# End of the first FFN: GpSimd's modulation-row additions and edge masks behind a new wait, the last rows scaled later

## The reference

```python
for i in range(DEPTH):
    mod_l = jnp.split((sc @ ada_w[i] + ada_b[i])[:, None, :], N_MOD, axis=-1)
    ...
    x = x + g_m * _rms_norm(y_lat, norm_post_mix[i])
    f_lat = _conv_ffn(_modulate(_rms_norm(x, norm_pre_ffn[i]), sh_f, sc_f),
                      ffn_w_up[i], ffn_conv_w[i], ffn_conv_b[i], ffn_w_down[i])
    x = x + g_f * _rms_norm(f_lat, norm_post_ffn[i])

def _conv_ffn(h, w_up, conv_w, conv_b, w_down):
    z = h @ w_up
    u, v = z[..., :D_FF], z[..., D_FF:]
    u = _dwconv(u, conv_w, conv_b, (1, 1))
    return (jax.nn.gelu(u) * v) @ w_down
```

## Time and profile before

| | |
|---|---|
| median of 3 runs | 1964.74 us (1964.59 to 1966.92) |
| profiled execution | 1965.58 us |
| its span | 1963.7 us |
| TensorE busy | 1923.5 us, 98% of the span |
| VectorE, GpSimd, ACT busy | 85%, 65%, 50% |

### The profile page before, as it was taken

The page is one execution under the profiler, slowest core; times in us unless marked ns, Lnnn a source line. Parts: engine busy times, 40 slices in busy tenths (PEclk is TensorE's granted clock), DMA queues, the critical chain, the costliest instruction groups (busy, mean ns, idle before and its releaser), DMA issues. The chain is left out here.

```text
span 1963.7 us, 28044 instructions
## 1 busy us (share of the span) xinstructions
PE 1923.5 (98%) x8838; PEld 1569.5 (80%) x8838; DVE 1661.0 (85%) x1752; ACT 991.1 (50%) x1417; POOL 1276.4 (65%) x858
## 2 busy tenths in 40 slices
PE   5999999999999999999999999999999999999999
PEld 3777776888888888888888789878888888888886
DVE  5688888879789889999989886897888888888887
ACT  5867678457444444445444456663434334333334
POOL 4534343665877788887778975475567655556765
PEclk9999999999999999999999999999999999999999
DMA  9322322541222232222332241111111111111114
GB/s 348 108 81 91 107 85 88 212 162 42 99 76 96 85 97 95 86 85 85 94 98 85 91 156 44 65 65 54 54 54 53 59 47 64 53 53 60 49 54 180
DMA packets 78017, 179.76 MB, mean 92 GB/s; under 512 B 5104, under 2 KB 28944, under 8 KB 77328
## 3 DMA queue, kind: packets, MB, share of 16 engines
q1 hardware_dynamic: 77968, 179.13, 26.9%
HBM read 166.52 MB, written 12.58 MB: 91 GB/s over the span
## 5 line engine op out<-in xcount | busy, mean ns | idle before, releaser
L2319 POOL TENSOR_TENSOR So_lo<-So_raw,So_hi 128x512 fp32r<-128x512 f32 x120 | 199.1, 1666 | 198.8 <-DVE So_raw L2962 167.7
L3026 DVE TENSOR_TENSOR Y<-Y,ps 128x1024 f32<-128x1024 f32 x280 | 324.2, 1208 | 3.3
L1836 ACT ACTIVATE So_hi<-So_raw 128x512 fp32r<-128x512 f32 x180 | 112.4, 624 | 148.2 <-POOL So_raw L2311 75.4
L2088 POOL TENSOR_TENSOR red<-red,E_quad 128x512 f32<-128x512 f32 x77 | 123.9, 1610 | 60.4 <-ACT E_quad L1890 57.5
L1836 ACT ACTIVATE WB_hi<-rawB 128x512 fp32r<-128x512 f32 x120 | 74.6, 629 | 166.0 <-PE ps L1258 111.8
L2041 POOL TENSOR_TENSOR WA_lo<-rawA,WA_hi 128x1024 fp32r<-128x1024 f32 x20 | 59.3, 2967 | 127.7 <-DVE u L2655 102.7
L1836 ACT ACTIVATE WA_hi<-rawA 128x512 fp32r<-128x512 f32 x120 | 73.1, 625 | 121.0 <-PE ps L1278 83.3
L1258 PE MATMUL ps<-T_hi,So_hi 128*128 128x512 f32 x336 | 131.3, 391 | 0.0
L1258 PE MATMUL ps<-T_hi,So_lo 128*128 128x512 f32 x336 | 130.8, 389 | 0.0
L1258 PE MATMUL ps<-H_hi,WA_hi 128*128 128x512 f32 x336 | 130.7, 389 | 0.0
L1258 PE MATMUL ps<-H_lo,WA_hi 128*128 128x512 f32 x336 | 130.7, 389 | 0.0
(11 more groups left out here) (445 smaller groups left out, 6270.6 us busy)
## 6 DMA issues: line engine op xcount, KB each, us to landing
rawA<-wA SPq DMA_DIRECT2D x62, 512.0 KB, 3.3
rawB<-wB SPq DMA_DIRECT2D x62, 512.0 KB, 3.4
E_quad<-ada SPq DMA_DIRECT2D x44, 512.0 KB, 3.5
quad<-ada SPq DMA_DIRECT2D x8, 2048.0 KB, 9.2
rawB<-wC SPq DMA_DIRECT2D x22, 512.0 KB, 3.7
rawA<-wC SPq DMA_DIRECT2D x20, 512.0 KB, 3.7
ada_first<-ada SPq DMA_DIRECT2D x8, 1024.0 KB, 14.9
outT<-X SPq DMA_DIRECT2D x16, 512.0 KB, 2.7
```

The costliest lines, as they stand in the source:

```text
L1836: A(dst[:, at:at + HF], op_source(name), ACT.Copy).then_inc(op_hi, 1)
L2088: TT(red[:], red[:], E_quad[:, :, k % 2 * P:k % 2 * P + P], ALU.add).then_inc(red_made, 1)
L2319: TT(lo[:, at:at + HF], op_source(name), hi[:, at:at + HF].bitcast(F32), ALU.subtract)\
L3026: TT(at, at, ps[:, bank:bank + 2, :], ALU.add).then_inc(d_added, 1)
```

## The change

On GpSimd (`last_step`), the first two additions of the last group (c = 2) wait for `last_ready` of the first half; the edge masks stay behind them. The other two (c = 3) are no longer in one piece behind the masks, but one each behind the two odd sums. On ACT, `scale_rows(PAIRS + 1, 3)` moves from behind the table load to behind the fourth square. On TensorE, `quad_columns` moves from behind n = 8 to behind n = 10.

```diff
@@ down_last (TensorE)
-                    if n == 8 and L == 0:
+                    if n == 10 and L == 0:
                         quad_columns(PAIRS + 1, ps[:, 3, 0:4])
                     if n == 10:
                         square_sums(q, 0)
@@ last_up (ACT)
                 act.preload_act_table(ACT.Sqrt)
-                if L == 0:
-                    scale_rows(PAIRS + 1, 3)
@@ ffn (ACT)
                 for n in range(2 * KT):
                     act.wait_ge(d_added, added + n + 1)
                     square(q, n // KT, n % KT, Y[:, n % KT, hs(n // KT)])
+                    if L == 0 and n == 3:
+                        scale_rows(PAIRS + 1, 3)
@@ add_rows (GpSimd)
-            def add_rows(q, c):
+            def add_rows(q, c, part=(0, 1)):
-                for k in (2 * c, 2 * c + 1):
+                for k in (2 * c + n for n in part):
@@ last_step (GpSimd)
                 if L == 0:
+                    pool.wait_ge(last_ready, 1)
                     add_rows(PAIRS + 1, 2)
                     window_edges()
-                    add_rows(PAIRS + 1, 3)
@@ ffn (GpSimd)
                 last_step(L)
                 q, i = 3 + 4 * L, 1 + 2 * L
-                odd_sums(q, 0)
+                for n, p in enumerate((3, 5)):
+                    odd_sum(q, 0, p)
+                    if L == 0:
+                        add_rows(PAIRS + 1, 3, (n,))
                 line_sums(q, 1, (1, 2, 3))
```

## The result

The changed kernel takes 1968.72 us (median of 20 runs, 1966.96 to 1971.47). The kernel before takes 1965.92 us in 20 runs beside it (1964.26 to 1967.71); the first three of them, shown ahead of the prediction, had a median 1.2 us lower, 1964.74. The ratio is 1.0013, 95% interval 1.0007 to 1.0019. The forecast was 1965.9, within 1963.6 to 1968.0. The sign was right, and the time lies 0.7 us outside the range.

What follows compares the result with a forecast made beforehand. TensorE, busy 1923.5 of 1963.7 us, was taken as the bound, so its idle or low-clock time decides. −1.2 (wait A) − 0.9 (quad_columns moved) + 3.3 (waiting before the sums) = +1.2 on 1964.74, giving 1965.9; range 1963.6 to 1968.0.

Steps and rivals of the forecast that it cites:

- Part 1: VectorE's gated product and second convolution, freed of GpSimd's additions, let TensorE start sooner: wait A falls by about 1.2 us.
- wait A: TensorE's 1.71 us idle before the first product with WB_hi, behind VectorE's convolution, gated product and remainder; to fall about 1.2.
- Part 2: TensorE finishes tiles 0 to 10 at 1134.9 instead of 1137.0, then waits for red's last addition (quad_columns) and last_sum.
- Part 3: GpSimd's queue starts 3.5 us later, its last addition directly ahead of VectorE's merge; last_sum at 1139.6, 1.2 us later.
- port shared by halves: Alternative to taking turns at SBUF: addition and merge would overlap, and merge would lose about 0.6 us instead of 1.2.
- Part 4: Behind last_sum: column sums at 1139.6 instead of 1138.4, then the same 1.6 us low-clock loss as before.
- Costs at nothing: Later pool_w load (ScalarE losing up to 2 us), X reload 3.5 us later, and later_coefs were taken to add nothing.
- The cover: shift_map and other tiles' column sums on TensorE hide ScalarE's wait for pool_w; without it, 2 us would be lost.
- Rival 1: The gain survives because last_sum ends no later than before: 1964.7 to 1963.7, or 1962.1 without low clock; chance 0.12.
- rival 4: The change does nothing: TensorE's wait for last_sum ends within 0.3 of where it did, 1964.7; chance 0.15.
- rival 3: Clearly slower: pool_w lands so late that shift_map and map scaling hold the last squares; 1968.9 and more; chance 0.04.
- Rival 2: Longer TensorE idleness makes the low clock last into tiles 12 to 15, costing another 1.6 us: 1967.5; chance 0.14.

Runs made afterwards that it cites:

- e6: The changed kernel with the last addition to red behind last_sum, quad_columns behind tile 11 and its readers behind tile 12; 1967.39 us, ratio 1.0009 to before.
- e5: The changed kernel with GpSimd's edge masks moved behind the last addition to red; 1965.59 us, ratio 1.0002 to before.
- e1: The changed kernel with 15 extra products keeping TensorE busy around quad_columns (12 ahead, 3 behind); 1966.46 us, ratio 1.0005 to before.
- e2: The kernel before with 6 extra products keeping TensorE busy ahead of the column sums behind tile 10; 1965.25 us, ratio 0.9994 to before.
- e8: The changed kernel with additions awaiting both remainder halves, masks, late additions, row scaling and quad_columns moved later, pool_w's load waiting for the last up products; 1965.77 us, ratio 0.9996.
- e4: The kernel before with only GpSimd's new wait for the remainder added; 1967.71 us, ratio 1.0011 to before.
- e9: e8 with pool_w's load ahead of the X reloads and GpSimd's first addition to X moved later; 1962.71 us, ratio 0.9985 to before.
- e3: The changed kernel without GpSimd's wait for the remainder, the other moves kept; 1965.98 us, ratio 1.0000 to before.
- e7: The kernel before with only GpSimd's edge masks moved behind the odd sums; 1964.63 us, ratio 0.9994 to before.

## Why the prediction was right up to the column sums and too low behind them

**Part 1, wait A: right.** Convolutions of 1.57 and 0.75 us (foreseen 1.6 and 0.7), idle time of 0.54 (0.6), first product with WB_hi at 1124.30 − 0.40 = 1123.90 (1123.9).

**Part 2: right.** TensorE came to its two waits at 1138.09 − 2.63 − 0.40 = 1135.06 (1134.9). That it would be idle twice there was wrong in form: quad_columns took 1.75 us to the start of the sums, and ended as last_sum did, so there was one idle time of 2.63.

**Part 3, GpSimd's queue: right to within 0.4 us at each step.** With the 0.40 off, the masks ended at 1131.65 (foreseen 1132.0; before, three of them took 0.77, 0.71 and 0.62 instead of 0.30, which is 1.2 us lost and not the 0.9 that was taken off), the first odd sum at 1133.0 (1133.2), the late addition at 1134.7 (1134.9), the second odd sum at 1136.0 (1136.1), the last addition at 1137.6 (1137.9), merge at 1138.2 (1138.4) and last_sum at 1139.4 (1139.6). Its place directly ahead of merge, and merge's price, are not only read from the timeline: e6 takes the addition away from there and merge returns to 0.69. The prediction's other claim, that the queue decides and not the squares, is shown by e5.

The Trainium skill, "SBUF — State Buffer", section "Who interferes with whom", had been set against a port shared by halves: it calls the port pair that VectorE shares with GpSimd an exclusive lock, and by that merge would wait out a whole addition. Merge took 1.64 with the addition of 1.71 ahead of it, and 0.69 without. The trace agrees.

**Part 4: the step that failed.** "I take the same 1.6 us loss" for the low clock. That was a loss read from one profile of before, and carried over to a TensorE that would be idle for far longer (4 us by the prediction's own count, 2.63 measured, 1.25 before), so the sum had the clock's change at nothing. What the runs show in its place:

- In the changed kernel the loss is 2.26 us (5.45 from the sums to tile 12 against 3.19 in e1). With 2.63 us idle, the clock had fallen before quad_columns began, so quad_columns and the sums too ran at half speed and not only what follows them. (Of quad_columns nothing is counted: the sums had to wait for last_sum, until 1139.79, in any case, and start as late in e1.) The clock was low for 6.8 us instead of 3.4, which the prediction itself had named as a sign of being wrong ("or if the low clock is absent or much longer").
- In the kernel before, the loss is 1.6 in the execution that was profiled (4.79 against 3.20; 3.17 in e2). Over the runs e2 puts it at about 0.8, with an interval that holds 1.6 and nothing alike. So by the two profiles the missing term is 5.45 − 4.79 = 0.66 us, and it is larger, up to 2.26, by as much as the runs of before lacked the low stretch.

Between the two profiles tile 12 is 1.04 + 0.66 = 1.70 later, of the 2.45 between the two profiled executions (1968.03 and 1965.58). The 0.40 came in ahead of the stretch: TensorE is 1.65 us ahead of before at 24 us, 0.38 ahead at 52 and 0.15 behind at 358, on either side of the two low stretches that the profile of before hasn't. The rest, 0.36, comes in between 1924 and 1928 us, at the end of the second FFN, where a 128x1024 convolution on VectorE takes 2.68 instead of 2.34; why was not tried.

With 0.8 for the loss of before, the sum would be 1.04 + 2.26 − 0.8 = 2.5 us, where the runs show 2.8. The clocks of the runs, recorded to three digits, point the same way. Their mean is 0.99590 over the 20 runs of the changed kernel and 0.99704 over the 83 runs of before beside the experiments. The difference, twice 0.00114 of 1966 us, is 4.5 us more at the lower level, where the two profiles differ by 3.4 in this stretch. But it also counts the stretches far ahead of the change, so the exact share is open.

**The anchor.** The prediction put its sum on "the median of the runs (1964.74)", which was that of three. All twenty have 1965.92. That is 1.2 us of the 2.8 by which the time exceeds the forecast. The other 1.6 is what the sum lacked: by the profiles 0.66 of it is the clock, by the medians of e2 nearly all (2.26 − 0.8). The last sum itself was well forecast, 1.04 later against 1.2.

**Costs at nothing.** Of pool_w, an issue at 1138.9 and a landing time of 7.4 were foreseen and up to 2 us of ScalarE's time. It was issued at 1139.99 and landed 6.2 later, and ScalarE waited 0.33 for it. The cover (shift_map and the column sums of other tiles) was not even drawn on. That it can fail is shown by e8, where everything ahead of shift_map is early: 1.31 us.

**The rivals.** Rival 1 (last_sum no later) is out by 1.04 us, rival 4 (nothing) by the ratio's interval, rival 3 by pool_w's landing. Rival 2 had the price that came nearest, 1967.5, and its condition was met: 6.8 us of low clock, more than twice the 2.7 in the earlier trace rows, though only twice the 3.4 that the clock was low in all before. Its place was wrong. It let the low level last into tiles 12 to 15, but tile 12 started at full clock; the stretch grew at its front, in which the sums lie. It deserved more than 0.14, since the prediction itself had TensorE idle for 4 us instead of 1.25.

## What to carry to other kernels

When an engine's work is moved out of the way of a chain, follow it to where it goes: here two additions left a convolution alone, and the last of them, pushed down its queue, stood directly ahead of the merge of a tree on which the same TensorE waited. Time in which TensorE stands still costs twice when the work behind it then runs at the lower clock, so a forecast needs a price for each of the two, and the price of the second must come from more than one execution. It also matters where the idle time lies: in e4 the low clock lay ahead of the last wait and cost nothing at the sums, in the changed kernel it lay behind that wait. A gain in front is had only after every other thing due at the same place is early too: first the sums (e8), then the load that shift_map needs (e9).

## What the runs showed of the hardware that had not been expected

- With about as much idle time, TensorE's clock falls in one execution and stays in another. It fell after 1.25 us idle in the profile of before, after 1.52 in e5 and after 1.97 in e4, and it stayed at 1.00 after 1.38 in e3, 1.17 in e4 and 0.58 in e7. It doesn't fall at once: in before, e5 and e4 TensorE had been at work again for 1.3, 1.3 and 2.2 us. After 2.63 and 3.41 us (changed, e6) it fell while the engine still stood idle.
- The low level lasted 3.4 us in before, e4 and e5 and 6.8 us in the changed kernel and e6, and no other length was met in this stretch. Why the near cases part was not found.
- One-column products pay for the clock like any other: eight take 0.94 to 1.05 us at the higher level, 1.87 at the lower.
- Of GpSimd's edge masks, a selection over 128x128 takes 0.29 or 0.30 us, and 0.63 where VectorE's operation stands ahead of it (up to 0.77 in before), while that one (1128.95, 0.77) loses at most 0.1 to the masks, against 0.69 of such additions alone. The masks wait for VectorE, but hardly hold it up, and still delay the odd sums queued behind them:

```profile
1128.89 0.29 POOL L2270 TENSOR_SCALAR_AFFINE_SELECT edge<-edge 128x128 f32<-128x128 f32 x1
1129.25 0.63 POOL L2273 TENSOR_SCALAR_AFFINE_SELECT edge<-edge 128x128 f32<-128x128 f32 x1
```
